# Last MLP chunk of a two-layer decoder trunk: two weight sums built in a second buffer, and the first product's weights moved to the staging buffer

## The chip, the core and the metric

One core of a Trainium2 chip runs the whole program. TensorE (PE) multiplies 128x128 weight tiles with up to 512 columns, VectorE (DVE) and ScalarE (ACT) do elementwise work, GpSimd (POOL) does some of it and issues DMAs that add to their destination, SyncE (SP) issues plain DMAs. The engines are ordered only by semaphores. The metric is the device time of one launch in microseconds.

## The reference

Two layers, 512 tokens, width 1024, all float32. Each layer has a token mixer (dilated attention and retention, merged by gates) and then an MLP, which is what matters here:

```python
h2 = rmsnorm(x, g_ffn)                                    # 512 x 1024
x = x + jnp.square(jax.nn.relu(h2 @ w_up)) @ w_down       # w_up 1024 x 4096, w_down 4096 x 1024
```

After the second layer a last RMSNorm makes the output.

## The kernel before

Every float32 product is made of three products of float32r operands: a value is split into a high part (a cast, on ACT) and a low part (value minus high part, on DVE), and PE adds high x high, low x high and high x low. Weights come in **units** of 128x2048 float32 (1 MB). A unit is loaded to a staging buffer `raw`, cast by ACT in two halves to `w_hi[n % 2]`, and DVE subtracts two halves into `w_lo[n % 2]`. The semaphore `lo_done` counts these halves. As there are two pairs `w_hi`/`w_lo`, the cast for unit n+1 may begin when unit n-1 is multiplied, that is when PE begins unit n. `raw` is single: the DMA of a half waits for the `lo_done` of the same half of the unit that used `raw` last (`load`, with `raw_before`).

The MLP is cut along the 4096 hidden columns into 4 chunks, c = 0 to 3. For a chunk, four U units make `us[c % 2]`, the squared ReLU (8 tiles of 512 columns, so 128x4096 float32), and the product with the chunk's 1024x1024 part of `w_down` is made by 7 block products D1 to D7 instead of 8, from sums of quarter blocks. With q(h, m) a quarter of the weights (`w_down_q[l, c, h, m]`, 1 MB), the weights that each product uses are:

- D1: q(0,0). D5: q(0,0)+q(0,1). D6: that + q(1,1). D4: that + q(1,0).
- D3: q(1,1). D7: q(1,1)+q(0,1).
- D2: q(1,0), which is the only one that goes through `raw`.

The first two rows are built in place in two buffers, `gh[0]` and `gh[1]`: SP loads the first quarter (`sum_slot`), ACT and DVE split it for its product, and when DVE is done POOL issues an accumulating DMA (`add_quarter`) that adds the next quarter to the buffer; then the next product's weights are split from it, and so on. POOL's DMAs stand in its program in a fixed order; for each chunk: the one for D5 (behind D1's split), for D6 (behind D5's), for D7 (behind D3's), for D4 (behind D6's).

The order of units (`M_SEQ`) interleaves the D products of chunk c with the U units of chunk c+1. The end of chunk 2 and the last chunk have no U units between them: D7 of chunk 2, U3, D2, D4 of chunk 2, and then, for chunk 3, `DOWN_LAST` = D1, D2, D5, D3, D6, D7, D4, each 24 matmuls of 512 columns. In the last chunk each product is done in two token halves (`down_halves`), each evicted on its own by DVE (`evict_half`, which adds the PSUM bank to an accumulator `acc`). PE begins D3 only when the first half of D5 is evicted, D7 when that of D6 is, D4 when that of D7 is, since they share PSUM banks (`down_ready`).

DVE's program for one unit of the last chunk is, in order: evict the second half of the unit before, split the weights of the unit after (`weights_low`), make the low parts of an activation operand (`a_low`), evict the first half of the own unit, and after D5 one sum of activations (`sum_of`). ACT's is: cast the weights of the unit after (`weights_high`), cast an activation operand (`a_high`). SP's program around this: the U loads of chunk 3, the first quarter for D1 of chunk 3, the load for D2 of chunk 2, the first quarter for D3 of chunk 3, the load for D2 of chunk 3, and then the next layer's first weights.

Of the kernel before, what the change touches and what calls it, by code (L numbers as in the profile page):

```python
# [52 lines left out]
def trunk(nc, a):  # L53
# [44 lines left out]
    LD = len(D_SEQ)  # L98
    LA = 2 * LD

    def by_raw(j):
        return j < M0 or M_SEQ[j - M0][0] == "U" or M_SEQ[j - M0][2] == 2

    RAW = [j for j in range(LU) if by_raw(j)]

# [7 lines left out]
    def m_unit(l, kind, c, i):  # L113
        return l * LU + M0 + M_SEQ.index((kind, c, i))

    def d_no(c, i):
        return D_SEQ.index((c, i))
# [7 lines left out]
    def slot_of(l, c, as_sum):  # L125
        return (l * CH + c) % 2 if as_sum else 1 - (l * CH + c) % 2

    def adds_before(l, c, as_sum):
        w, s = l * CH + c, slot_of(l, c, as_sum)
        return w // 2 * 4 + ((3 if s == 0 else 1) if w % 2 else 0)  # L130

    with ExitStack() as ctx:
        def sb(name, shape, dt):
# [5 lines left out]
        def sem(name):  # L139
            return ctx.enter_context(nc.semaphore(name))  # L140
# [95 lines left out]
            a_sets[r] = (at("M", f"a_hi{r}", [P, 4, 2 * P], F32R), at("M", f"a_lo{r}", [P, 4, 2 * P], F32R))  # L236
        acc = [at("M", "acc0", [P, TB, S], F32), tables]
        us = [at("M", f"u{i}", [P, KT, S], F32) for i in range(2)]
        assert top["M"] == pad
        top["res_lo"], top["res_hi"] = zone0, zone0 + 3 * KT * S * 4  # L240
        res_hi = at("res_hi", "res_hi", [P, KT, S], F32R)
# [152 lines left out]
        u_done = sem("u_done")  # L394
        sum_in = [sem(f"sum_in{i}") for i in range(2)]
        sum_added = [sem(f"sum_added{i}") for i in range(2)]
        a_sum = sem("a_sum")
        a_hi_done = sem("a_hi_done")
        a_ready = sem("a_ready")
# [59 lines left out]
        def _(sp):  # L459
# [35 lines left out]
            for l in range(0, DEPTH):  # L495
# [135 lines left out]
                for i in range(0, 2):  # L631
                    for u in range(O_U):
                        load(l * LU + O0 + i * O_U + u, cols(w_o_u[l], 2 * i + u))
                def quarter(c):
                    d = raw[:].rearrange("p (k c) -> p k c", k=4)
                    return [(d[:, m:m + 2, :], w_down_q[l, c, 1, 0][:, m:m + 2, :]) for m in (0, 2)]

                def sum_slot(c, as_sum):
                    w, slot = l * CH + c, slot_of(l, c, as_sum)
# [17 lines left out]
                for c in range(CH):  # L657
                    if c < CH - 1:
                        up_weights(c + 1, 1)
                        up_weights(c + 1, 2)  # L660
                        up_weights(c + 1, 3)
                        sum_slot(c + 1, True)
                    load(m_unit(l, "D", c, 2), quarter(c))
                    if c < CH - 2:
                        up_weights(c + 2, 0)
                    if c < CH - 1:
                        sum_slot(c + 1, False)
# [9 lines left out]
        def _(act):  # L677
# [9 lines left out]
                    nc.scalar.copy(w_hi[s][:, c], raw[:, c]).then_inc(hi_done, 1)  # L687

            def hi_sum(l, c, i, n):
                slot = slot_of(l, c, i in (1, 5, 6, 4))  # L690
                adds = {1: 0, 5: 1, 6: 2, 4: 3, 3: 0, 7: 1}[i]
                if adds == 0:
                    act.wait_ge(sum_in[slot], (l * CH + c) * 16 + 16)
                else:
                    act.wait_ge(sum_added[slot], (adds_before(l, c, i in (1, 5, 6, 4)) + adds) * 16)
                for h in HALVES:
                    nc.scalar.copy(w_hi[n % 2][:, h], gh[slot][:, h]).then_inc(hi_done, 1)  # L697
# [75 lines left out]
            for l in range(0, DEPTH):  # L773
# [215 lines left out]
                def weights_high(j):  # L989
                    n = l * LU + M0 + j  # L990
                    act.wait_ge(mm_done, n * 2 - 2 + MM_CREDIT)
                    if j < len(M_SEQ):
                        kind, c, i = M_SEQ[j]
                        if kind == "D" and i != 2:
                            hi_sum(l, c, i, n)
                            return
                    hi_halves(n, n % 2)
# [94 lines left out]
        @block.gpsimd  # L1092
        def _(pool):
            nc.gpsimd.memset(ones[:], 1.0).then_inc(const_set, 1)
            nc.gpsimd.memset(inv_d[:], 1.0 / D).then_inc(const_set, 1)
            nc.gpsimd.memset(eps[:], EPS).then_inc(const_set, 1)
            nc.gpsimd.memset(shares[:], 0.0).then_inc(const_set, 1)
            for l in range(0, DEPTH):
                for i in range(0, PAIRS):
                    J = l * PAIRS + i  # L1100
                    q = l * LQ + i * P_U
                    for u in range(4):
                        for o in range(2):
                            pool.wait_ge(bank_free[o], q + u + 1 + BANK_CREDIT)
                            pool.wait_ge(rot_out, J * 8 + 2 * u + o + 1)
                            pool.wait_ge(tables_done, l + 1)
                            nc.gpsimd.tensor_tensor(rcos[:], rot[:], cosA if u < 3 else cosR,  # L1107
                                                    ALU.mult).then_inc(rot_cos, 1)

                def add_quarter(c, behind, as_sum, h, m):  # L1110
                    slot = slot_of(l, c, as_sum)
                    pool.wait_ge(lo_done, m_unit(l, "D", c, behind) * 2 + 2 + UNIT_CREDIT)
                    pool.wait_ge(sum_in[slot], (l * CH + c) * 16 + 16)
                    nc.gpsimd.dma_start(gh[slot][:].rearrange("p (k c) -> p k c", k=4), w_down_q[l, c, h, m],  # L1114
                                        accum_op=ALU.add).then_inc(sum_added[slot], 16)

                for c in range(CH):
                    add_quarter(c, 1, True, 0, 1)
                    add_quarter(c, 5, True, 1, 1)
                    add_quarter(c, 3, False, 0, 1)  # L1120
                    add_quarter(c, 6, True, 1, 0)


        @block.vector
        def _(dve):
# [108 lines left out]
            for l in range(0, DEPTH):  # L1234
# [350 lines left out]
                def weights_low(j):  # L1585
                    n = l * LU + M0 + j
                    if j < len(M_SEQ):
                        kind, c, i = M_SEQ[j]
                        if kind == "D" and i != 2:
                            for hf in range(2):  # L1590
                                lo_half(n, n % 2, hf, gh[slot_of(l, c, i in (1, 5, 6, 4))])
                            return
                    lo(n, n % 2)

# [73 lines left out]
                for j, (kind, c, i) in enumerate(M_SEQ):  # L1668
                    last_chunk = kind == "D" and c == CH - 1
                    if j > 0:  # L1670
                        before = M_SEQ[j - 1]
                        if before[0] == "U":
                            relu_square(before[1], before[2], 1)
                        elif before[1] == CH - 1:
                            evict_half(before[2], 1)
                        else:
                            evict(before[1], before[2])
                    if kind == "U" and c > 0:
                        for t in ((5,), (3,), (7,), ())[i]:
                            sum_of(c - 1, t)  # L1680
                    if last_chunk and i == 2:
                        sum_of(c, 3)
                    if j + 1 < len(M_SEQ) or not last_layer:
                        weights_low(j + 1)
                    if j == 0:
                        rms_squared(l)
                    if kind == "U" and c > 0:
                        for t in ((5,), (3, 6), (7, 2), (4,))[i]:
                            a_low(c - 1, t)
                        if i == 0:  # L1690
                            sum_of(c - 1, 6)
                    if (kind, i) in (("U", 2), ("U", 3)) and (c == 0) == (i == 2):
                        a_low(c, 1)
                    if (kind, c, i) == ("U", 0, 2) and last_layer:
                        gains_diag()
                    if (kind, c, i) == ("D", CH - 2, 2):
                        sum_of(CH - 1, 5)
                    if (kind, c, i) == ("D", CH - 2, 4):
                        a_low(CH - 1, 2)
                        sum_of(CH - 1, 6)  # L1700
                    if last_chunk:
                        for t in {1: (5,), 2: (3,), 5: (6,), 3: (7,), 6: (4,)}.get(i, ()):
                            a_low(c, t)
                        if i != 4:
                            evict_half(i, 0)
                        if i == 5:
                            sum_of(c, 7)
                    if kind == "U":
                        relu_square(c, i, 0)
                    if last_chunk and last_layer and i == 7:  # L1710
                        f_add(0, 2, 4)
                        f_inverse(0, 2, 1)
                        dve.wait_ge(g_kept, 2)
                        f_scaled(0, 1)
                        f_scaled(0, 0)
# [542 lines left out]
```

## Time and profile before

| | us |
|---|---|
| median of 3 runs (lowest, highest) | 1888.55 (1887.93, 1889.95) |
| the profiled execution | 1888.48 |
| its span in the trace | 1886.4 |
| PE busy in it | 1865.5 (99%) |
| DVE / ACT / POOL busy | 1255.6 / 837.2 / 129.4 |

The span runs from the first to the last instruction of the trace. The profile's times below are microseconds from the span's start. A MATMUL row shows 0.39 us, but matmuls overlap: at full clock their starts are 0.23 us apart, so a D product takes 5.44 us and the gap between one row's start and the next shows a stall. Layer 0's last chunk runs from 896.21 us, layer 1's from 1834.79 us.

### The profile page before, as it was taken

Reading aid. Unit: us, or ns where it says so; the run is one execution under the profiler, and the core shown is the slowest. Engines: PE = TensorE matmul, PEld = TensorE weight load, DVE = VectorE, ACT = ScalarE, POOL = GpSimd, SP = SyncE. Lnnn points to the kernel's source line nnn. Section 1 sums busy time; section 2 is a strip of 40 time slices with the busy share of each in tenths; the row PEclk is TensorE's granted clock in tenths of the full one; section 3 lists DMA queues with packets and bytes.
Section 4 is the critical chain, followed back from the end, with each engine's and each line's share of the span. In section 5 each row is a group of like instructions: output and inputs, shape, how many; then the busy total and the mean of one; then the engine's idle time right before and its main releaser. Section 6 shows DMA issues by size and latency. Waiting matters only on the chain.

```text
span 1886.4 us, 22990 instructions
## 1 busy us (share of the span) xinstructions
PE 1865.5 (99%) x9064; PEld 1549.7 (82%) x9064; DVE 1255.6 (67%) x1858; ACT 837.2 (44%) x1234; POOL 129.4 (7%) x104
## 2 busy tenths in 40 slices
PE   9999999999999999999899999999999999999997
PEld 7888888887888888888788888888878888888886
DVE  5356778767456666767863568788665575676777
ACT  7325465464223333434472255554632233344344
POOL 0001111100000000000000112111000000000100
PEclk9999999999999999999999999999999999999999
DMA  4543233333333465564626333233243334655655
GB/s 146 200 159 120 83 89 118 90 93 104 120 101 114 132 134 136 150 136 125 145 88 240 96 104 104 77 118 104 68 146 101 101 112 113 141 148 134 134 147 121
DMA packets 208235, 230.64 MB, mean 122 GB/s; under 512 B 13440, under 2 KB 160640, under 8 KB 207360
## 3 DMA queue, kind: packets, MB, share of 16 engines
q1 hardware_dynamic: 190512, 194.74, 32.7%
q0 software_dynamic: 16896, 33.56, 10.5%
q8 instruction: 72, 1.18, 0.2%
q10 hardware_dynamic: 720, 0.87, 0.1%
q14 instruction: 35, 0.29, 0.0%
HBM read 215.38 MB, written 13.77 MB: 121 GB/s over the span
## 4 chain that ended last, share of the span: by engine, by line
PE 85%; issue 6%; DVE 4%; DMA 3%; ACT 2%; POOL 0%; SPq 0%; POOLq 0%; ACTq 0%; DVEq 0%
PE pj L1816 19%; PE pj L1818 19%; PE pj L1817 19%; DMA gh<-in_w_down 2%; PE yr L2122 1%; PE yr L2124 1%; PE yr L2126 1%; DVE w_lo L1140 1%; PE pt L2122 1%; PE pt L2124 1%; PE pt L2126 1%; PE sc L2122 1%; PE sc L2124 1%; PE sc L2126 1%; PE yr L1923 1%
## 5 line engine op out<-in xcount | busy, mean ns | idle before, releaser
L1816 PE MATMUL pj<-h_hi,w_hi 128*128 128x512 f32 x1408 | 554.4, 394 | 1.0 <-DVE sA L1515 1.0
L1818 PE MATMUL pj<-h_hi,w_lo 128*128 128x512 f32 x1408 | 548.5, 390 | 0.0
L1817 PE MATMUL pj<-h_lo,w_hi 128*128 128x512 f32 x1408 | 548.3, 389 | 0.0
L1140 DVE TENSOR_TENSOR w_lo<-w_raw,w_hi 128x1024 fp32r<-128x1024 f32 x279 | 329.9, 1220 | 115.1 <-ACT w_hi L687 113.6
L687 ACT CAST w_hi<-w_raw 128x1024 fp32r<-128x1024 f32 x276 | 278.6, 1049 | 270.5 <-PE pj L1818 56.9
L1816 PEld LDWEIGHTS pj<-h_hi,w_hi 128*128 128x128 f32 x1408 | 264.4, 188 | 59.0 <-issue 1.9
L1818 PEld LDWEIGHTS pj<-h_hi,w_lo 128*128 128x128 f32 x1408 | 264.3, 188 | 56.0
L1817 PEld LDWEIGHTS pj<-h_lo,w_hi 128*128 128x128 f32 x1408 | 264.5, 188 | 53.9 <-issue 0.5
L697 ACT CAST w_hi<-gh 128x1024 fp32r<-128x1024 f32 x96 | 96.0, 1050 | 118.2 <-DMA gh<-in_w_down 50.5
L1107 POOL TENSOR_TENSOR rcos<-rot,tables 128x512 f32<-128x512 f32 x64 | 87.6, 1370 | 692.4 <-ACT rot L808 633.8
L1140 DVE TENSOR_TENSOR w_lo<-gh,w_hi 128x1024 fp32r<-128x1024 f32 x96 | 113.1, 1219 | 14.2 <-ACT w_hi L697 14.0
L975 ACT ACTIVATE relu<-pj 128x512 f32<-128x512 f32 x64 | 38.2, 597 | 189.6 <-PE pj L1818 189.6
L1581 DVE TENSOR_TENSOR u<-relu,rstd_all 128x512 f32<-128x512 f32 x64 | 44.0, 688 | 105.5 <-ACT relu L975 105.5
L1114 POOL DMA_DIRECT2D gh<-in_w_down x32 | 41.2, 1286 | 1038.4 <-DVE w_lo L1140 1038.4
L808 ACT COPY rot<-pj 128x512 f32<-128x512 f32 x48 | 27.9, 582 | 110.5 <-PE pj L1818 64.5
L2122 PE MATMUL sc<-w_hi,a_hi 128*128 128x512 f32 x160 | 63.3, 396 | 5.7 <-DVE a_lo L1623 3.4
L1288 DVE TENSOR_TENSOR swp<-swp,tables 128x512 f32<-128x512 f32 x64 | 65.4, 1022 | 4.4 <-ACT swp L812 2.7
L2126 PE MATMUL sc<-w_hi,a_lo 128*128 128x512 f32 x160 | 63.0, 394 | 0.0
L2124 PE MATMUL sc<-w_lo,a_hi 128*128 128x512 f32 x160 | 62.9, 393 | 0.0
L2122 PE MATMUL yr<-w_hi,a_hi 128*128 128x512 f32 x160 | 62.2, 389 | 0.0
L2124 PE MATMUL yr<-w_lo,a_hi 128*128 128x512 f32 x160 | 62.2, 389 | 0.0
L2126 PE MATMUL yr<-w_hi,a_lo 128*128 128x512 f32 x160 | 62.2, 389 | 0.0
(339 smaller groups left out, 3102.4 us busy)
## 6 DMA issues: line engine op xcount, KB each, us to landing
w_raw<-in_w_in SPq DMA_DIRECT2D x151, 512.0 KB, 4.7
w_raw<-in_w_up SPq DMA_DIRECT2D x64, 512.0 KB, 4.9
gh<-in_w_down POOLq DMA_DIRECT2D x32, 1024.0 KB, 8.7
gh<-in_w_down SPq DMA_DIRECT2D x16, 1024.0 KB, 5.1
w_raw<-in_w_b SPq DMA_DIRECT2D x16, 512.0 KB, 3.9
w_raw<-in_w_o SPq DMA_DIRECT2D x16, 512.0 KB, 3.9
w_raw<-in_w_down SPq DMA_DIRECT2D x16, 512.0 KB, 4.5
x_scratch<-x SPq DMA_DIRECT2D x2, 2048.0 KB, 10.1
```

The source lines that it names most:

```text
L687: nc.scalar.copy(w_hi[s][:, c], raw[:, c]).then_inc(hi_done, 1)
L697: nc.scalar.copy(w_hi[n % 2][:, h], gh[slot][:, h]).then_inc(hi_done, 1)
L1107: nc.gpsimd.tensor_tensor(rcos[:], rot[:], cosA if u < 3 else cosR, ALU.mult).then_inc(rot_cos, 1)
L1140: nc.vector.tensor_tensor(w_lo[s][:, c], src[:, c], w_hi[s][:, c], ALU.subtract).then_inc(lo_done, 1)
L1288: nc.vector.tensor_tensor(swp[:], swp[:], sinA if u < GROUPS else sinR, ALU.mult).then_inc(rot_sin, 1)
L1581: nc.vector.tensor_tensor(to, relu[:, o, :], rstd_all[:], ALU.mult).then_inc(relu_scaled, 1)
L1816: nc.tensor.matmul(out, w_hi[s][:, wc], acts[0], start=first, stop=False)
L1817: nc.tensor.matmul(out, w_hi[s][:, wc], acts[1], start=False, stop=False)
L1818: return nc.tensor.matmul(out, w_lo[s][:, wc], acts[0], start=False, stop=last)
L2122: nc.tensor.matmul(out, hi[:, k, t], w_hi[s][:, w], start=opens and k == 0, stop=False, skip_group_check=not opens)
L2124: nc.tensor.matmul(out, hi[:, k, t], w_lo[s][:, w], start=False, stop=False, skip_group_check=not opens)
L2126: return nc.tensor.matmul(out, lo[:, k, t], w_hi[s][:, w], start=False, stop=k == 3, skip_group_check=not opens)
```

## The change

It touches the last chunk of each layer only.

- `us[0]`, which held chunk 2's activations, has no use in the last chunk. Its two halves of 1 MB become `spares[7]` and `spares[4]`.
- The weights of D7 and D4 of chunk 3 are built there: SP loads q(1,1) to `spares[7]` and q(0,0) to `spares[4]` when the last operand has been made from `us[0]` (D4 of chunk 2), and POOL adds one quarter to the first and three to the second, each waiting for the one before it.
- D1 of chunk 3 (q(0,0)) is loaded to `raw` like D2, right after D2 of chunk 2, and is so counted among the `raw` users. `gh[...]` with q(0,0) serves D5 and D6 only, with two adds, and the first of them does not wait for D1's split. D3's buffer has no add.
- POOL's order for chunk 3 is: add for D5, first add of `spares[4]`, the add of `spares[7]`, second and third add of `spares[4]`, add for D6.
- In DVE's program for the last chunk the eviction of the own unit's first half goes ahead of `a_low`.

```diff
+    def plain(c, i):
+        return i == 2 or (c, i) == (CH - 1, 1)
+
     def by_raw(j):
-        return j < M0 or M_SEQ[j - M0][0] == "U" or M_SEQ[j - M0][2] == 2
+        return j < M0 or M_SEQ[j - M0][0] == "U" or plain(*M_SEQ[j - M0][1:])
...
+        spare = us[(CH - 2) % 2]
+        spares = {7: spare[:, 0:4, :].rearrange("p k c -> p (k c)"), 4: spare[:, 4:8, :].rearrange("p k c -> p (k c)")}
...
-                    load(m_unit(l, "D", c, 2), quarter(c))
+                    load(m_unit(l, "D", c, 2), quarter(c, 1))
+                    if c == CH - 2:
+                        load(m_unit(l, "D", c + 1, 1), quarter(c + 1, 0))
+                        sp.wait_ge(a_ready, l * LD + d_no(c, 4) + 1)
+                        for i, src in ((7, w_down_q[l, c + 1, 1, 1]), (4, w_down_q[l, c + 1, 0, 0])):
+                            sp.dma_start(spares[i].rearrange("p (k c) -> p k c", k=4), src).then_inc(spare_in[i], 16)
...
             def hi_sum(l, c, i, n):
+                if c == CH - 1 and i in (7, 4):
+                    act.wait_ge(spare_added[i], (l + 1) * 16 * {7: 1, 4: 3}[i])
+                    for h in HALVES:
+                        nc.scalar.copy(w_hi[n % 2][:, h], spares[i][:, h]).then_inc(hi_done, 1)
+                    return
...
                 def add_quarter(c, behind, as_sum, h, m):
                     slot = slot_of(l, c, as_sum)
-                    pool.wait_ge(lo_done, m_unit(l, "D", c, behind) * 2 + 2 + UNIT_CREDIT)
+                    if not plain(c, behind):
+                        pool.wait_ge(lo_done, m_unit(l, "D", c, behind) * 2 + 2 + UNIT_CREDIT)
                     pool.wait_ge(sum_in[slot], (l * CH + c) * 16 + 16)
...
-                for c in range(CH):
+                def add_spare(i, n, h, m):
+                    if n == 0:
+                        pool.wait_ge(spare_in[i], l * 16 + 16)
+                    else:
+                        pool.wait_ge(spare_added[i], (l * 3 + n) * 16)
+                    nc.gpsimd.dma_start(spares[i].rearrange("p (k c) -> p k c", k=4), w_down_q[l, CH - 1, h, m],
+                                        accum_op=ALU.add).then_inc(spare_added[i], 16)
+
+                for c in range(CH - 1):
                     add_quarter(c, 1, True, 0, 1)
                     add_quarter(c, 5, True, 1, 1)
                     add_quarter(c, 3, False, 0, 1)
                     add_quarter(c, 6, True, 1, 0)
+                add_quarter(CH - 1, 1, True, 0, 1)
+                add_spare(4, 0, 0, 1)
+                add_spare(7, 0, 0, 1)
+                add_spare(4, 1, 1, 1)
+                add_spare(4, 2, 1, 0)
+                add_quarter(CH - 1, 5, True, 1, 1)
...
                     if last_chunk:
+                        if i != 4:
+                            evict_half(i, 0)
                         for t in {1: (5,), 2: (3,), 5: (6,), 3: (7,), 6: (4,)}.get(i, ()):
                             a_low(c, t)
-                        if i != 4:
-                            evict_half(i, 0)
```

Left out: the semaphores `spare_in` and `spare_added`, `adds_before` with the new counts, and the places where DVE and ACT ask `plain(c, i)` instead of `i == 2`, and DVE takes `spares[i]` as the source for D7 and D4.

## Rows read from the trace of the kernel before

**Rows 1.** The page: busy time, share, instructions.

```profile
PE 1865.5 (99%) x9064; PEld 1549.7 (82%) x9064; DVE 1255.6 (67%) x1858; ACT 837.2 (44%) x1234; POOL 129.4 (7%) x104
```

**Rows 2.** Timeline of PE, layer 0: first matmuls of D2 D5 D3 D6 D7 D4.

```profile
901.65 0.39 PE L2122 MATMUL yr<-w_hi,a_hi 128*128 128x512 f32 x1
907.09 0.39 PE L2122 MATMUL pt<-w_hi,a_hi 128*128 128x512 f32 x1
...
914.41 0.47 PE L2122 MATMUL pt<-w_hi,a_hi 128*128 128x512 f32 x1 [1.72 <-DVE a_lo L1623]
919.98 0.39 PE L2122 MATMUL sc<-w_hi,a_hi 128*128 128x512 f32 x1
927.15 0.47 PE L2122 MATMUL sc<-w_hi,a_hi 128*128 128x512 f32 x1 [1.57 <-DVE a_lo L1623]
934.35 0.47 PE L2122 MATMUL sc<-w_hi,a_hi 128*128 128x512 f32 x1 [1.48 <-DVE tables L1647]
```

**Rows 3.** Timeline of DVE: a_lo of D4 (chunk 2) and D1; D1's split; D5's eviction.

```profile
879.90 2.35 DVE L1623 TENSOR_TENSOR a_lo<-u,a_hi 128x1024 fp32r<-128x1024 f32 x2
...
892.17 2.35 DVE L1140 TENSOR_TENSOR w_lo<-gh,w_hi 128x1024 fp32r<-128x1024 f32 x2
...
913.64 0.68 DVE L1647 TENSOR_TENSOR tables<-tables,pt 128x512 f32<-128x512 f32 x1
```

**Rows 4.** Timeline of POOL: adds for D5, D6, D7, D4.

```profile
894.82 1.28 POOL L1114 DMA_DIRECT2D gh<-in_w_down  x1 [41.47 <-DVE w_lo L1140]
908.08 1.28 POOL L1114 DMA_DIRECT2D gh<-in_w_down  x1 [11.98 <-DVE w_lo L1140]
912.88 1.28 POOL L1114 DMA_DIRECT2D gh<-in_w_down  x1 [3.51 <-DVE w_lo L1140]
920.80 1.30 POOL L1114 DMA_DIRECT2D gh<-in_w_down  x1 [6.64 <-DVE w_lo L1140]
```

**Rows 5.** Timeline of ACT: D6's cast and D7's.

```profile
916.84 2.00 ACT L697 CAST w_hi<-gh 128x1024 fp32r<-128x1024 f32 x2 [6.60 <-DMA gh<-in_w_down]
...
921.88 2.01 ACT L697 CAST w_hi<-gh 128x1024 fp32r<-128x1024 f32 x2 [2.08 <-DMA gh<-in_w_down]
```

**Rows 6.** The chain of waits: start, us, what.

```profile
863.04 4.94 DMA gh<-in_w_down
...
920.80 9.34 DMA gh<-in_w_down
```

**Rows 7.** The page, DMA issues: xcount, size, median us to landing.

```profile
gh<-in_w_down POOLq DMA_DIRECT2D x32, 1024.0 KB, 8.7
```

**Rows 8.** Timeline of SP: D2's load (chunk 2); D3's quarter; D2's load.

```profile
872.42 1.50 SPq L475 DMA_DIRECT2D w_raw<-in_w_down  x2
889.88 0.37 SPq L645 DMA_DIRECT2D gh<-in_w_down  x1
890.31 1.00 SPq L475 DMA_DIRECT2D w_raw<-in_w_down  x2
```

**Rows 9.** DMA view of 852 to 864 us, 40 slices of 0.3 us.

```profile
GB/s 0 0 0 0 0 0 20 75 55 102 177 184 205 198 198 191 205 198 218 212 212 218 218 171 263 181 266 335 386 386 379 386 382 382 362 215 10 0 0 0
...
w_raw<-in_w_up SPq DMA_DIRECT2D x2, 512.0 KB, 6.9
```

**Rows 10.** Timeline of SP and POOL: what was issued in that window.

```profile
852.07 1.28 POOL L1114 DMA_DIRECT2D gh<-in_w_down  x1 [9.23 <-DVE w_lo L1140]
...
855.33 1.56 SPq L475 DMA_DIRECT2D w_raw<-in_w_up  x2
```

**Rows 11.** Timeline of PE, layer 1: D7, two later matmuls, D4's second half.

```profile
1865.67 0.47 PE L2122 MATMUL sc<-w_hi,a_hi 128*128 128x512 f32 x1 [1.86 <-DVE a_lo L1623]
...
1867.94 0.63 PE L2122 MATMUL sc<-w_hi,a_hi 128*128 128x512 f32 x1
1868.37 0.63 PE L2124 MATMUL sc<-w_lo,a_hi 128*128 128x512 f32 x1
...
1876.52 0.50 PE L2122 MATMUL sc<-w_hi,a_hi 128*128 128x512 f32 x1 [0.83 <-DVE tables L1647]
```

More of the change, by code:

```diff
@@ L126, in slot_of, with adds_of @@
         return (l * CH + c) % 2 if as_sum else 1 - (l * CH + c) % 2
+    def adds_of(c, as_sum):
+        return (2 if as_sum else 0) if c == CH - 1 else (3 if as_sum else 1)
     def adds_before(l, c, as_sum):
-        w, s = l * CH + c, slot_of(l, c, as_sum)
-        return w // 2 * 4 + ((3 if s == 0 else 1) if w % 2 else 0)
+        slot = slot_of(l, c, as_sum)
+        return sum(adds_of(w % CH, slot_of(0, w, True) == slot) for w in range(l * CH + c))
     with ExitStack() as ctx:
@@ L396, in trunk @@
         sum_added = [sem(f"sum_added{i}") for i in range(2)]
+        spare_in = {i: sem(f"spare_in{i}") for i in (7, 4)}
+        spare_added = {i: sem(f"spare_added{i}") for i in (7, 4)}
         a_sum = sem("a_sum")
@@ L633, in _, with quarter @@
                         load(l * LU + O0 + i * O_U + u, cols(w_o_u[l], 2 * i + u))
-                def quarter(c):
+                def quarter(c, h):
                     d = raw[:].rearrange("p (k c) -> p k c", k=4)
-                    return [(d[:, m:m + 2, :], w_down_q[l, c, 1, 0][:, m:m + 2, :]) for m in (0, 2)]
+                    return [(d[:, m:m + 2, :], w_down_q[l, c, h, 0][:, m:m + 2, :]) for m in (0, 2)]
                 def sum_slot(c, as_sum):
@@ L993, in weights_high @@
                         kind, c, i = M_SEQ[j]
-                        if kind == "D" and i != 2:
+                        if kind == "D" and not plain(c, i):
                             hi_sum(l, c, i, n)
@@ L1588, in weights_low @@
                         kind, c, i = M_SEQ[j]
-                        if kind == "D" and i != 2:
+                        if kind == "D" and not plain(c, i):
                             for hf in range(2):
-                                lo_half(n, n % 2, hf, gh[slot_of(l, c, i in (1, 5, 6, 4))])
+                                lo_half(n, n % 2, hf, spares[i] if c == CH - 1 and i in (7, 4) else
+                                        gh[slot_of(l, c, i in (1, 5, 6, 4))])
                             return
```

## The prediction

> **What bounds the kernel now.** The page says PE: busy 1865.5 us [rows 1] of a span of 1886.4. So a change can only win where PE stands still. I read PE's own timeline next. A D product is 24 matmuls; D2 and D5 begin 5.44 us apart (901.65, 907.09), which is the unstalled pitch [rows 2]. After them D3 begins at 914.41 where 912.53 was due, a stall of 1.88; D6 at 919.98 (as it should, 5.57 later); D7 at 927.15, 7.17 after D6, a stall of 1.73; D4 at 934.35, 7.20 after D7, a stall of 1.76 [rows 2]. Unstalled, D4 would begin at 901.65 + 5 x 5.44 = 928.85, so this layer's last chunk holds 5.5 us that can be won.
>
> What ends those waits? For D3 the reader must not stop at the releaser: the last thing was the eviction of D5's first half, at 913.64 for 0.68 us [rows 3]; that half was multiplied by 907.09 + 2.72 = 909.8 already, and DVE was behind with other work. For D4 the chain of waits shows POOL's add issued at 920.80 and 9.34 us to its landing at 930.14 [rows 6], though PE had begun D7 at 927.15 and ACT could have cast D4's weights from then on. For D6 ACT waited for a DMA until 916.84, for D7 until 921.88 [rows 5]: these sums arrive just in time or somewhat late. In layer 1 D7 begins at 1865.67 after 1.86 us of standing, and a while later the matmuls start 0.43 us apart instead of 0.23: the granted clock is at the 1.2 GHz level there [rows 11]. Layer 0, with stalls of the same size, shows no such drop.
>
> **What DMAs cost here.** An accumulating DMA of 1 MB takes 8.7 us from issue to landing, alone [rows 7]. Two in a row: the adds issued at 908.08 and 912.88 [rows 4] landed where ACT's casts begin, 916.84 and 921.88 [rows 5], that is 5.1 us apart. So one occupies the DMA engines for 5.1 us, and the one behind it lands 5.1 us after it. A plain load moves about 386 GB/s in the DMA view where an accumulating one moves about 205 [rows 9]; 1.05 MB / 386 is 2.7 us of the engines, and it lands 4.94 after its issue [rows 6]. The same view shows what both do together: the accumulating DMA was issued at 852.07, two halves of a plain load from 855.33 on [rows 10]; the rate stays near 205 until about 859 and is 386 only from 860.4 on, and the plain halves took 6.9 us to land [rows 9]. The two do not overlap to any gain: their times on the engines add, and the plain load stood behind the whole accumulating one.
>
> **The change part by part.** Times are those of layer 0; layer 1 lies 938.5 later (D7 927.15, 1865.67).
>
> (a) Add for D5. It was issued at 894.82 behind D1's split [rows 4]; now it waits only for its first quarter, landed at 863.04 + 4.94 = 868.0 [rows 6]. POOL had been idle for 41.47 us before 894.82 [rows 4], so it goes at 868 and occupies the engines from about 870 to 875.5. That covers D2 of chunk 2's load, issued at 872.42 [rows 8], which slips by some 1.2 us. PE needs it only for 885.33 on my count (three products before 901.65: 901.65 - 3 x 5.44), so it costs PE nothing. But DVE's split of it, and with it the a_lo pair that starts at 879.90 [rows 3], slips by 1.2 too.
>
> (b) `spares`. SP waits for the first of that pair: 879.90 + 1.2 + 1.2 = 882.3. In front are the two halves of D1's load, issued when D2's halves are split, with 2.7 us of transfer ending near 884.1. Then two plain MB: 884.1 + 2 x 2.7 = 889.5, landing near 890.0.
>
> (c) POOL's queue, the heart of it. From 890 the DMA engines get: D3's quarter, issued at 889.88 as before [rows 8] (2.7); first add to `spares[4]`, issued at 890.0 (5.1); the add to `spares[7]`, issued one POOL instruction, 1.28 us [rows 4], later (5.1); D2's load (2.7). The first add lands at 890.0 + 8.7 + 2.1 for the part of D3's quarter in front of it = 900.8, the one for D7 at 905.9. The second add to `spares[4]` may be issued only at 900.8 and finds D7's add and D2's load before it: 900.8 + 5.1 + 2.7 + 5.1 = 913.7. The third is issued at 913.7, and **only behind it in POOL's program comes the add for D6**, which was issued at 908.08 before. The third has idle engines, 8.7, and lands at 922.4; D6's add lands 5.1 later, at 927.5. Before, it landed at 916.8.
>
> (d) D2's load. It used `raw` behind chunk 2's D2 and was issued at 890.31 [rows 8]; now `raw` holds D1's weights until DVE has split them, 892.17 to 894.52 [rows 3], so its halves go at 893.4 and 894.6, among POOL's adds. The engines' work listed in (c) is 15.6 us from 891.7 on, so the second half lands at up to 908. Cast (1.0), split (1.2) and handovers make 2.4 us to 910.5, and PE can do D2's last three quarters after that: it ends at 910.5 + 0.75 x 5.44 = 914.6 where it ended at 907.09. A PE stall of 7.5 us. D5 then begins at 915.6 (its split stands behind D2's in DVE's program), D3 near 922 and ends near 928. The Trainium skill, "DMA: Bandwidth & Descriptors", Queues, rings and completion order, says that each DMA engine goes round between the queues at packet granularity, 9 to 17 descriptors typically; by that rule D2's second half would land at 905.5 and D2 end at 912. In the window above no such switch is seen. It changes nothing in the sum, only the margin by which (e) decides instead of (d).
>
> (e) PE after the change. D6 begins 2.4 us after its sum landed, at 929.9 (D3 is done at 928). D7 waits for the eviction of D6's first half, which in DVE's program stands behind D6's second split (1.1), eviction, a_lo, eviction, D7's split (0.7 + 1.1 + 0.7 + 2.35), and takes 0.7: 6.7 us, so D7 begins at 936.6. D4's weights have been there since 922.4 and its split and the eviction of D7's first half fit in D7's 5.44 us: D4 begins at 942.0 without a stall. Before it was 934.35: **7.7 us late**. What follows D4 (turns, the next layer, in layer 1 the last norm with D4's second half at 1876.52 behind DVE [rows 11]) hangs on D4's start by the same work as before.
>
> (f) The eviction ahead of `a_low`: would give D3 the 1.14 us of one DVE instruction of that size (half of 2.35 [rows 3]). It lies in the shadow of (c): 0. D5's add, D7's and D4's sums come in time, and are worth 0 too, since D6 stands before them.
>
> (g) Clock. A stall of 1.86 us was followed by a drop in one layer and not in the other; stalls of 5 to 7 us make a drop likelier. With the drop of [rows 11] D7 took from 1865.67 to about 1873.0, 7.3 instead of 5.44, so at most 1.9 us a drop; at least 0, as D2's drop has D3's margin of 2 us to vanish in. Between 0 and 3 us in all; I take 0.5.
>
> Sum: 2 x 7.7 + 0.5 = 15.9 on the profiled execution's 1888.48 (its span 1886.4 and 2.1 around it); the median shown is 1888.55, the same within 0.1. That is 1904.
>
> **Rivals.**
>
> *It does what it is built for: 1878.* If the three adds and the two spares were done soon enough, all stalls from D3 to D4 go: 5.5 in layer 0 and in layer 1 as much (D4 began about 1873.0 there: 1876.52 less the stall of 0.83 and half a product, 2.72 [rows 11]; unstalled 938.5 + 928.85 = 1867.4); 1888.5 - 11 = 1877.5, say 1878. For it: D5's, D7's and D4's sums are in truth taken off the path. Against: D6's add stands last in POOL's order and cannot be issued before two further adds have landed one after the other; it needs accumulating DMAs that cost the engines half of what [rows 5] show.
>
> *No contention: 1892.* If (a)'s slip is nil and neither D3's quarter nor D2's load delays POOL's adds: first add 888.8 + 8.7 = 897.5, D7's 902.6, second 907.7, third 916.4, D6's 921.5; D6 begins at 923.9, D7 at 930.6, D4 at 936.0, 1.7 late; 1888.5 + 3.4 = 1892. With D7's wait for DVE gone as well, 1.3 less a layer, 1889. Against it: the plain megabytes must go through the same engines [rows 9].
>
> *Plain loads starve: 1920.* If POOL's queue is served first as long as it has work, D3's quarter and D2's load go only in the gaps of POOL's chain; D2's second half would land near 919, D5's split be done near 928, D6's add (it waits for that) be issued there and land at 937: D6 at 939.3, 9.4 later than in (e), twice: 1904 + 19 = 1923, less if one half slips in. For it: [rows 9], where the plain load waits for the whole accumulating one. Against: one waiting behind another that began first is no priority.
>
> **Chances.** The forecast's case, 1897 to 1912: 0.62. Faster, 1878: 0.12. No contention: 0.13, of which half lies within 0.2% (3.8 us, about what a measurement of this kernel can tell from no change). Starving: 0.10; the rest anything else. So faster 0.12, same 0.08, slower 0.80. The range leaves out the case of 1878 and the worst of starving: 1889 to 1915.
>
> **What would show it.** Right: on POOL two adds near 900.8 and 913.7 and then at once D6's; D6's cast near 927 waiting for that DMA; PE standing for 5 to 8 us in or before D2 with the w_raw cast behind a DMA; D3's eviction no longer what PE waits for; D4 without a wait. Wrong: adds landing 5 us after their issue; D2's cast near 897 as before; D6's wait on D3's end. If D5's add is not seen near 868, (a) is wrong and with it the time of everything behind it.

## The result and the profile after

| | before | changed |
|---|---|---|
| median of 4 runs each, us (lowest, highest) | 1888.24 (1887.38, 1889.95) | 1914.14 (1912.96, 1914.91) |
| the profiled execution, us | 1888.48 | 1914.91 |
| its span, us | 1886.4 | 1912.8 |
| ratio to before, 95% interval | | 1.0135 (1.0118 to 1.0153) |

The changed kernel is 26 us slower. The forecast was 1904, range 1889 to 1915: the median lies inside the range by 0.9 us and above 1897 to 1912, which the prediction called the forecast's own case.

Where the 26.4 us of span are. PE's timeline of layer 0's last chunk, first matmuls of D2, D2's second quarter (the first to need the second half of its weights), D5, D3, D6, one later matmul, D4 (the numbers in brackets are us of waiting and the releaser); [rows 2] are their like:

```profile
901.11 0.39 PE L2158 MATMUL yr<-w_hi,a_hi 128*128 128x512 f32 x1
...
905.40 0.50 PE L2158 MATMUL yr<-w_hi,a_hi 128*128 128x512 f32 x1 [2.77 <-DVE w_lo L1175]
...
910.09 0.47 PE L2158 MATMUL pt<-w_hi,a_hi 128*128 128x512 f32 x1 [0.31 <-DVE w_lo L1175]
...
916.38 0.47 PE L2158 MATMUL pt<-w_hi,a_hi 128*128 128x512 f32 x1 [0.59 <-issue]
...
935.13 0.76 PE L2158 MATMUL sc<-w_hi,a_hi 128*128 128x512 f32 x1 [12.74 <-DVE w_lo L1175]
...
936.97 0.63 PE L2160 MATMUL sc<-w_lo,a_hi 128*128 128x512 f32 x1
...
947.67 0.39 PE L2158 MATMUL sc<-w_hi,a_hi 128*128 128x512 f32 x1
```

From D2's start to D4's it was 32.7 us [rows 2] and is 46.6: 13.9 lost. The largest piece is the wait of 12.74 ahead of D6; the shorter waits in D2, D5 and D3 (3.7 together) and the slow matmuls behind D6's (1.7) come to about what the old stalls had cost, 5.5. D4 follows without a wait, as does D7. Why D6 waits is read on POOL: the add for D5, the two first spare adds (`u<-` is the dead buffer), the second and the third to `spares[4]`, the add for D6 (`gh<-` again):

```profile
867.88 1.28 POOL L1135 DMA_DIRECT2D gh<-in_w_down  x1 [15.07 <-DMA gh<-in_w_down]
893.60 2.59 POOL L1143 DMA_DIRECT2D u<-in_w_down  x2 [24.44 <-DMA u<-in_w_down]
907.03 1.30 POOL L1143 DMA_DIRECT2D u<-in_w_down  x1 [10.84 <-DMA u<-in_w_down]
919.05 1.29 POOL L1143 DMA_DIRECT2D u<-in_w_down  x1 [10.71 <-DMA u<-in_w_down]
919.79 1.85 POOL L1135 DMA_DIRECT2D gh<-in_w_down  x1
```

and on ACT, D2's two casts and D6's:

```profile
897.34 1.05 ACT L702 CAST w_hi<-w_raw 128x1024 fp32r<-128x1024 f32 x1 [3.95 <-DMA w_raw<-in_w_down]
903.04 1.04 ACT L702 CAST w_hi<-w_raw 128x1024 fp32r<-128x1024 f32 x1 [4.65 <-DMA w_raw<-in_w_down]
...
932.68 1.99 ACT L717 CAST w_hi<-gh 128x1024 fp32r<-128x1024 f32 x2 [19.88 <-DMA gh<-in_w_down]
```

The load of D2's second half stands on SP at:

```profile
894.01 0.37 SPq L485 DMA_DIRECT2D w_raw<-in_w_down  x1
```

The add for D6 was issued at 908.08 [rows 4] and is at 919.79, less than a microsecond behind the third spare add. Of these 11.7 us D5's own lateness explains 3.3 (its split ended at 911.08, 907.79 before); for the rest the add stands behind two landings in POOL's program. The chain of waits (start, us, what) now runs over these DMAs:

```profile
883.62 9.71 DMA u<-in_w_down
...
893.60 12.95 DMA u<-in_w_down
...
919.79 12.81 DMA gh<-in_w_down
```

In layer 1 it is the same picture, smaller (POOL's two first spare adds, the second, the third, the add for D6):

```profile
1848.57 2.62 POOL L1143 DMA_DIRECT2D u<-in_w_down  x2 [23.55 <-DMA u<-in_w_down]
1861.06 1.28 POOL L1143 DMA_DIRECT2D u<-in_w_down  x1 [9.86 <-DMA u<-in_w_down]
1871.17 1.28 POOL L1143 DMA_DIRECT2D u<-in_w_down  x1 [8.84 <-DMA u<-in_w_down]
1871.92 1.84 POOL L1135 DMA_DIRECT2D gh<-in_w_down  x1
```

There D2 waits 4.39 and D6 7.46, and from D1's start (1851.46) to D4's second half it takes 51.5 us where it took 41.7, 9.8 lost. The rest is a wait that the change does not touch in the code, a gate unit (weights of the token mixer's gates) in layer 1, with a matmul pitch of 0.43 behind it. First D2, D6 and D4's second half of layer 1, then that unit:

```profile
1862.82 0.50 PE L2158 MATMUL yr<-w_hi,a_hi 128*128 128x512 f32 x1 [4.39 <-DVE w_lo L1175]
...
1887.20 0.76 PE L2158 MATMUL sc<-w_hi,a_hi 128*128 128x512 f32 x1 [7.46 <-DVE w_lo L1175]
...
1902.98 0.50 PE L2158 MATMUL sc<-w_hi,a_hi 128*128 128x512 f32 x1 [0.25 <-DVE tables L1683]
```

```profile
1408.23 0.50 PE L1852 MATMUL pj<-h_hi,w_hi 128*128 128x512 f32 x1 [2.26 <-DVE sA L1550]
...
1410.33 0.63 PE L1853 MATMUL pj<-h_lo,w_hi 128*128 128x512 f32 x1
```

13.9 + 9.8 + 3.3 there (1.7 of wait more than the 0.59 that this unit waited before, and 8 matmuls 0.2 us longer each), less 0.5 by which this execution ran ahead before the chunk, is the 26.4 to within 0.2.

### The profile page after: what moved, and what is told of

It reads as the page before. It is cut to its first block, busy times and chain, and to the rows that moved or that the text cites. A ratio compares the mean times of both kernels' runs of the same rounds, so it can differ in the third digit from the quotient of the medians.

```text
span 1912.8 us, 22996 instructions
## 1 busy us (share of the span) xinstructions
PE 1871.6 (98%) x9064; PEld 1553.4 (81%) x9064; DVE 1255.5 (66%) x1858; ACT 836.8 (44%) x1234; POOL 134.9 (7%) x108
## 4 chain that ended last, share of the span: by engine, by line
PE 87%; DMA 5%; DVE 3%; ACT 2%; issue 2%; POOL 0%; SPq 0%; ACTq 0%; DVEq 0%; POOLq 0%
PE pj L1852 19%; PE pj L1854 19%; PE pj L1853 19%; DMA u<-in_w_down 2%; PE sc L2158 1%; PE sc L2160 1%; PE sc L2162 1%; PE yr L2158 1%; PE yr L2160 1%; PE yr L2162 1%; DMA gh<-in_w_down 1%; PE pt L2158 1%; PE pt L2162 1%; PE pt L2160 1%; DVE w_lo L1175 1%
## 5 line engine op out<-in xcount | busy, mean ns | idle before, releaser
L1175 DVE TENSOR_TENSOR w_lo<-w_raw,w_hi 128x1024 fp32r<-128x1024 f32 x283 | 334.9, 1220 | 134.8 <-ACT w_hi L702 133.4
L702 ACT CAST w_hi<-w_raw 128x1024 fp32r<-128x1024 f32 x280 | 282.7, 1049 | 296.1 <-PE pj L1854 56.9
L717 ACT CAST w_hi<-gh 128x1024 fp32r<-128x1024 f32 x84 | 83.9, 1049 | 109.9 <-DMA gh<-in_w_down 52.4
L1175 DVE TENSOR_TENSOR w_lo<-gh,w_hi 128x1024 fp32r<-128x1024 f32 x84 | 99.0, 1220 | 24.1 <-ACT w_hi L717 23.8
L1135 POOL DMA_DIRECT2D gh<-in_w_down x28 | 37.1, 1325 | 944.5 <-DVE w_lo L1175 914.3
```

Of the source, the lines that this page charges most:

```text
L1175: nc.vector.tensor_tensor(w_lo[s][:, c], src[:, c], w_hi[s][:, c], ALU.subtract).then_inc(lo_done, 1)
```

## Experiments

Times are medians; ratios are to the kernel before, run beside each on the same chip (its medians there: 1887.65 to 1888.28). "Before" and "changed" in the table say which of the two kernels was edited.

| kernel | us | ratio, 95% interval |
|---|---|---|
| changed | 1914.14 | 1.0135 (1.0118 to 1.0153) |
| e2: changed, D6's add ahead of the third spare add | 1895.21 | 1.0041 (1.0026 to 1.0056) |
| e4: changed, D1 in gh again | 1920.45 | 1.0177 (1.0161 to 1.0192) |
| e8: e2 and e4 together | 1902.02 | 1.0073 (1.0057 to 1.0088) |
| e5: changed, no spare adds (sums incomplete) | 1880.46 | 0.9966 (0.9955 to 0.9978) |
| e9: changed, next layer's weights later | 1910.99 | 1.0123 (1.0109 to 1.0136) |
| e3: before, D1 through raw | 1889.84 | 1.0008 (0.9998 to 1.0018) |
| e1: before, evictions ahead of a_low | 1887.59 | 0.9998 (0.9989 to 1.0007) |
| e6: e1, D4's sum in the dead buffer | 1893.48 | 1.0027 (1.0016 to 1.0039) |
| e7: e1, D6's sum in the dead buffer | 1896.28 | 1.0044 (1.0031 to 1.0056) |
| e10: before, two evictions ahead of the split | 1886.78 | 0.9996 (0.9987 to 1.0005) |

**e2, the order on POOL.**

```diff
                 add_spare(4, 1, 1, 1)
-                add_spare(4, 2, 1, 0)
                 add_quarter(CH - 1, 5, True, 1, 1)
+                add_spare(4, 2, 1, 0)
```

> The changed kernel with one line moved: POOL issues the add for D6 ahead of the third add to spares[4], not behind it. Theory (POOL's order): D6's add is then issued when D5 is split, near 911 us of layer 0, and lands near 923 instead of 932.6; D6 begins near 925.5 instead of 935.1, the third add lands near 929 and D4 follows without a long wait: about 9 us a layer back, 1896. Rival (D2's late load and the busy DMA engines set the end): D6's add lands only 2 or 3 us earlier, since the bytes ahead of it are the same, and the time stays at 1908 or more.

Measured 1895.21: two lines exchanged give 19 us back. POOL's timeline of e2, the second spare add, D6's, the third:

```profile
906.89 1.30 POOL L1143 DMA_DIRECT2D u<-in_w_down  x1 [10.95 <-DMA u<-in_w_down]
912.67 1.29 POOL L1135 DMA_DIRECT2D gh<-in_w_down  x1 [4.47 <-DVE w_lo L1175]
919.38 1.28 POOL L1143 DMA_DIRECT2D u<-in_w_down  x1 [5.42 <-DMA u<-in_w_down]
```

D6's add now waits for DVE's split of D5, as it was meant to, and ACT's cast of D6 began at 924.24. The rival (the same bytes ahead, so 2 or 3 us) is out: the place in POOL's program counted, worth 19 of the 26 us.

**e4, D1 in gh again.**

```diff
-        return i == 2 or (c, i) == (CH - 1, 1)
+        return i == 2
...
-                        load(m_unit(l, "D", c + 1, 1), quarter(c + 1, 0))
```

> The changed kernel with D1's weights of the last chunk taken from gh again, so that D2's load goes early and the add for D5 waits for D1's split; both spares and POOL's order stay. Theory (POOL's order): the stall in D2 (3.2 us in layer 0, 4.8 in layer 1) goes, but D6's sum still lands near 932, so the end hardly moves: 1911 to 1916. Rival (D2's late load carries the loss): 4 to 8 us a layer come back, 1900 to 1906.

Measured 1920.45, slower than either theory had it. PE's timeline of e4, D2, D5, D3, D6:

```profile
901.15 0.39 PE L2157 MATMUL yr<-w_hi,a_hi 128*128 128x512 f32 x1
...
906.60 0.39 PE L2157 MATMUL pt<-w_hi,a_hi 128*128 128x512 f32 x1
...
912.26 0.47 PE L2157 MATMUL pt<-w_hi,a_hi 128*128 128x512 f32 x1
...
938.03 0.77 PE L2157 MATMUL sc<-w_hi,a_hi 128*128 128x512 f32 x1 [19.81 <-DVE w_lo L1174]
```

D2's stall is gone, and D6 begins 2.9 us later than in the changed kernel. Taking the stall in D2 away gave nothing back. What costs more instead is read on POOL (the add for D5, the two first spare adds, the second):

```profile
894.32 1.28 POOL L1134 DMA_DIRECT2D gh<-in_w_down  x1 [41.47 <-DVE w_lo L1174]
895.06 3.15 POOL L1142 DMA_DIRECT2D u<-in_w_down  x2
912.05 1.30 POOL L1142 DMA_DIRECT2D u<-in_w_down  x1 [13.83 <-DMA u<-in_w_down]
```

The add for D5, at 894.32 instead of 868, stands in front of the spare adds, and the second of these goes out 5.0 us later than in the changed kernel. D1 through raw, with the early add that it allows, saves 6 us in all; that the early add is what saves them is read from these rows, and no run moves it alone. Some of the 6 is clock: behind the longer wait 13 matmuls start 0.43 us apart, 7 in the changed kernel.

**e8, both edits.**

> The changed kernel with both of two edits tried alone before: D1's weights in gh again, and D6's add ahead of the third spare add. Theory (D6 is set by when POOL can issue its add, which is behind the landing of the second spare add's predecessor, not by D2): with the add for D5 in front at 894 the second spare add is issued near 912 and D6's at 913.3, landing near 923, as with the new order alone: 1893 to 1898. Rival (D2's stall and the order each cost their part, and the parts add): 1888 or less.

Measured 1902.02, above the theory's 1893 to 1898 and the rival's 1888: the expectation failed. The order gives 19 us with D1 in raw (1914.14 to 1895.21) and 18 with it in gh (1920.45 to 1902.02); D1 in raw saves 6 us in one order and 7 in the other. The two add up, with the sign of the second opposite to the rival's. Where the theory failed is D6's landing, put at 923: its cast began at 927.28, since its add, issued at 912.78 as expected, went out right behind the second spare add at 912.03 (in e2 5.8 us behind it).

**e5, the spare adds left out.** Of the sums for D7 and D4 only one quarter is there.

```diff
-                    act.wait_ge(spare_added[i], (l + 1) * 16 * {7: 1, 4: 3}[i])
+                    act.wait_ge(spare_in[i], (l + 1) * 16)
...
-                add_spare(4, 0, 0, 1)
-                add_spare(7, 0, 0, 1)
-                add_spare(4, 1, 1, 1)
-                add_spare(4, 2, 1, 0)
```

> The changed kernel without the four accumulating DMAs into the spares: D7 and D4 take one plain quarter each, so the result leaves out parts of their sums. Everything else, the plain loads to the spares and D2's late load among it, stays. Theory (the chain of spare adds in front of D6's add): D2's load lands near 899 and stalls nothing much, D6's add is issued when D5 is split and lands near 917, no product waits for more than 1 us, D4 begins near 928.5: 1878. Rival (the plain loads to the spares and D1 through raw cost on their own): above 1890.

Measured 1880.46, 2.5 us above the theory's figure and far from the rival's. So the four adds a layer cost the changed kernel 34 us in all. With them gone it is 8 us faster than the kernel before, plain loads to the spares and D1 through raw included: that is what lay to be won had the adds been free (11 by my rival's sum). It issues two adds a layer in the last chunk where the kernel before issues four, so some of the 8 us may be work that no full kernel can leave out. Even here D3 and D7 began late behind a DVE eviction, by 0.2 and 0.8 us. ACT's timeline of e5, D2's two casts and D6's:

```profile
897.56 1.05 ACT L702 CAST w_hi<-w_raw 128x1024 fp32r<-128x1024 f32 x1 [3.91 <-DMA w_raw<-in_w_down]
899.11 1.06 ACT L702 CAST w_hi<-w_raw 128x1024 fp32r<-128x1024 f32 x1 [0.50 <-DMA w_raw<-in_w_down]
...
915.99 2.00 ACT L717 CAST w_hi<-gh 128x1024 fp32r<-128x1024 f32 x2 [6.03 <-DMA gh<-in_w_down]
```

The second of D2's halves is there 3.9 us earlier than in the changed kernel, where spare adds are under way beside it.

**e9, another megabyte out of the way.**

```diff
                     if c < CH - 1:
                         sum_slot(c + 1, False)
+                if l < DEPTH - 1:
+                    sp.wait_ge(lo_done, m_unit(l, "D", CH - 1, 6) * 2 + 2 + UNIT_CREDIT)
```

> The changed kernel, with the next layer's first weights (1 MB, which go out while the spare adds run in layer 0) held back until D6's weights are split. Theory (every megabyte in front of D6's add delays it by its time on the DMA engines): D6's sum in layer 0 lands 2.5 to 3.5 us earlier, layer 1, which has no such load, stays: 1911. Rival (only the order of POOL's landings counts, plain loads fit between): no change, 1914.

Measured 1910.99, 3 us less, but the two ratios' intervals overlap, so the medians alone do not tell it from the changed kernel. The profiled executions do: the third spare add of layer 0 goes out at 917.30 instead of 919.05 and D6's cast at 931.24 instead of 932.68, while D1 had begun 0.45 later than there, so 1.9 us are won in this place. The changed kernel's own layer 1, which has no next layer to load for, says the same: its second spare add is followed by the third 10.1 us later (1861.06, 1871.17), in layer 0 it takes 12.0 (907.03, 919.05). The direction is the theory's, the size less than its 2.5 to 3.5 us.

**e3, D1 through raw alone.** The changed kernel's `plain`, its load of D1 and its early add for D5, on the kernel before; no spares.

> The kernel before with one part of the change: D1 of the last chunk through raw, and the add for D5 at once; no spares, D7's and D4's sums in their old buffers, the eviction in its old place. Theory: D2's load goes at 893 but finds free engines and lands near 898.5, no stall; D5's split can be 2.5 us earlier and with it D6's add and split, and so D4's add, which bounds D4: 0 to 2 us a layer won, 1885 to 1888. Rival (D1 through raw makes D2 late by itself): 2 or more lost a layer, 1892 or more.

Measured 1889.84, the interval holds 1: no change, 2 us above what the theory had. The second half of D2 was cast at 899.63, in time; but the add for D6 was issued at 908.17, as before (908.08), so an earlier D5 sum moved nothing. DVE no longer waited for it, but D2's second half was split at 900.71, 1.7 us later than before, and the work behind that pushed D5's split to 905.51, where it had been (905.43).

**e1, the evictions alone.**

```diff
+                        if i != 4:
+                            evict_half(i, 0)
                         for t in {1: (5,), 2: (3,), 5: (6,), 3: (7,), 6: (4,)}.get(i, ()):
                             a_low(c, t)
-                        if i != 4:
-                            evict_half(i, 0)
```

> The kernel before with one part of the change: in DVE's program for the last chunk the eviction of the own unit's first half goes ahead of a_low. Theory (a product waits for the later of its sum and the eviction): D3 and D7 begin 1.1 us earlier each, D7 then bound by its sum, which lands at 921.9; D4's sum still lands near 930.1, so D4 begins as before: within 1 us, 1887 to 1888.5. Rival (each eviction moved earlier moves the end): 2 us a layer won, 1884.

Measured 1887.59, no difference: within the theory's range, away from the rival's. PE's timeline of e1, D3, D7, D4:

```profile
912.63 0.47 PE L2122 MATMUL pt<-w_hi,a_hi 128*128 128x512 f32 x1 [0.37 <-issue]
...
925.56 0.47 PE L2122 MATMUL sc<-w_hi,a_hi 128*128 128x512 f32 x1 [1.29 <-issue]
...
932.83 0.47 PE L2122 MATMUL sc<-w_hi,a_hi 128*128 128x512 f32 x1 [1.55 <-DVE tables L1647]
```

D3 begins 11.4 us after D2 (12.8 before [rows 2]), D4 31.6 after it (32.7 before): of 1.4 us won at D3, 1.1 is left at D4, and of that nothing that the medians can tell.

**e6 and e7, one spare only.** Both have D1 in gh and e1's evictions. e6 builds D4's sum in the dead buffer, e7 D6's, with D4's made in the old buffer right after D5. POOL's order in e7, where the last wait is for the add before it in `gh`, and D4's second add follows:

```diff
                 add_spare(0, 0, 1)
                 add_quarter(c, 1, True, 0, 1)
                 add_spare(1, 1, 1)
                 add_quarter(c, 5, True, 1, 1)
                 add_quarter(c, 3, False, 0, 1)
                 pool.wait_ge(sum_added[slot], (adds_before(l, c, True) + 2) * 16)
...
```

> The kernel before with the eviction first and only D4's sum built in the dead buffer, three adds, in POOL's order: first spare add, D5's, second spare add, D6's, D7's, third spare add; D1 stays in gh, D7's sum stays in its old buffer. Theory (an add delays what stands behind it by 5.1 us of the DMA engines, and by the landing that POOL waits for): D6's add is issued near 909 and lands near 918, D7's near 923, the third spare add near 928: D4 begins 2 us earlier than before, 1884. Rival (any spare adds ahead of D6's cost more than they bring): 1890 or more.

> The kernel before with the eviction first and only D6's sum built in the dead buffer (two adds), D4's in the buffer of D5 by two adds right after D5's split, so that no add waits for D6's split; POOL's order: first spare add, D5's, second spare add, D4's first, D7's, D4's second. Theory: D6's sum lands near 909, D7's near 922, D4's near 927; D3 and D6 begin on time, D7 within 1.5 us and D4 within 1.5 us of unstalled: 4 us a layer won, 1880. Rival (the DMA engines are too busy with one more megabyte and one more add): the adds land 5 us later than that and nothing is won, 1887 or more.

Measured 1893.48 and 1896.28: both theories failed, at the same place, and both times lie where the rivals had them. ACT's timeline of e7, D2's two casts:

```profile
900.14 1.05 ACT L694 CAST w_hi<-w_raw 128x1024 fp32r<-128x1024 f32 x1 [6.40 <-DMA w_raw<-in_w_down]
903.96 1.05 ACT L694 CAST w_hi<-w_raw 128x1024 fp32r<-128x1024 f32 x1 [2.77 <-DMA w_raw<-in_w_down]
```

D2's load was issued at 890.12, where it always was, and behind D3's quarter as always; new ahead of it is the first spare add (886.85). Before, the first cast was at 896.67. PE stood for 0.96 and 2.10 us in D2 (2.17 and 2.41 in e6), D5's split came 4 to 7 us later than before, and D6's or D4's add with it: D4 started 36 us after D1's end in both, where it had been 32.7. I had counted what the spare add does to the adds behind it, and not to D2's plain load.

**e10, DVE's order without any spare.** For D6 and D7 the eviction of the first half goes ahead of the split of the next weights.

```diff
+                    if last_chunk and i in (6, 7):
+                        evict_half(i, 0)
                     if j + 1 < len(M_SEQ) or not last_layer:
                         weights_low(j + 1)
...
```

The other products' evictions stand ahead of `a_low`, as in e1.

> The kernel before, with no spares and its own adds; only DVE's program changes: the eviction of D6's and of D7's first half goes ahead of the split of the next product's weights, that of the others ahead of a_low. Theory (with the sums landing near 921.4 and 928.7, D7 and D4 wait for an eviction that stands behind the whole split): D7 begins when D6 ends, near 924.0 instead of 925.6 with the eviction only ahead of a_low, and D4 near 931.0 (landing 928.7 plus one half cast and split) instead of 932.8: 3 us a layer before the kernel before, 1884. Rival (D4's sum sets D4 and DVE has no part in it): as with the eviction ahead of a_low alone, 1887.5.

Measured 1886.78; the interval holds 1, and of the 4 us forecast at most 1 is there. That is nearer to the rival's 1887.5 than to the theory's 1884. In layer 0 it did what it should: D7 follows D6 with no wait, and D4 stands only for its own split, 30.25 us after D2 instead of 32.7:

```profile
931.24 0.47 PE L2124 MATMUL sc<-w_hi,a_hi 128*128 128x512 f32 x1 [1.34 <-DVE w_lo L1140]
```

In layer 1 D4 began 30.9 us after D2 instead of 32.6, and lost it again:

```profile
1867.88 0.76 PE L2124 MATMUL sc<-w_hi,a_hi 128*128 128x512 f32 x1 [2.71 <-DVE w_lo L1140]
...
1873.79 0.50 PE L2124 MATMUL sc<-w_hi,a_hi 128*128 128x512 f32 x1 [1.48 <-DVE tables L1647]
```

Its sum arrived no earlier, so PE stood 2.71 us for it; 8 matmuls behind that wait start 0.43 us apart, the 1.7 us that the kernel before lost in D7 [rows 11]; and its second half waited 1.48 us for D7's second eviction (0.83 before), which on DVE stands behind work of the last norm. That half began 36.8 us after D2, 36.3 before. So this is the fastest of the kernels that compute the whole, and not one that a measurement tells from the kernel before.

## Why the prediction held

The sign, the place and the mechanism were right, the size was short: 15.9 us forecast, 26 measured (26.4 of span in the profiled execution). Of the 10.5 us between 15.9 and 26.4, layer 0 holds 6.2 (13.9 against 7.7), layer 1 2.1 (9.8 against 7.7), and 3.3 are the gate unit's, which the prediction does not have; against these go the 0.5 of clock that (g) had in the sum and the 0.5 of the earlier start. That the time still fell into the range owes something to its width.

- (a) held in its main point: the add for D5 went out at 867.88, 868 forecast.
- (c) was the heart, and e2 shows it: D6's add behind two landings and a third add. Its parts, forecast and measured in layer 0: spare loads landed 890.0 and 893.3; second spare add issued 900.8 and 907.0; third 913.7 and 919.0; D6's sum landed 927.5 and 932.6. The first two links are 6.2 us late; from there to the end it took 26.7 and 25.6.
- That last agreement is partly luck. From the third add on the price was right, 13.8 us against 13.6 here and 13.5 in layer 1. The step before it was forecast at 12.9, with the add for D7 and D2's load in front; it took 12.0 in layer 0 beside the next layer's first weights, which the list in (c) left out, and 10.1 in layer 1 without them.
- The first late link: the two spare megabytes. I let them follow D1's load at the engines' pace. They took 9.7 us from issue, with D3's quarter (issued 889.34) beside them on SP's queue. They were also issued at 883.21 and not 882.3: (a)'s slip of D2's load of chunk 2 was not 1.2 but 2.6 us (DVE's a_lo pair at 881.96, after 0.5 for the earlier start of this execution).
- The second: from the first spare add to the next on its buffer it took 13.4 us and not 10.8. D2's load, which (c) put behind both adds, went out with them, its halves at 892.88 and 894.01, and the next layer's first megabyte began at 899.68. In layer 1, without the latter, it is 12.5, so most of the excess is not the next layer's. How much is D2's load's no run separates.
- (d) was wrong in size and in meaning. D2's first half left ahead of the adds; its second left at 894.01, 0.4 us behind the first spare add, and was cast at 903.04, not past 908, 3.5 us before that add landed. So the loads did not queue up behind whole adds as (d) added them; its other figure, by turns between the queues, was 905.5. PE stood 2.77 us in D2, not 7.5, and D5 began at 910.09, not 915.6. e4 removes the stall and the kernel becomes slower: it lay in D6's shadow, as (e) had it, and D1 through raw with its early add, which (f) priced at 0, was worth 6 us.
- (e): D6 to D4 12.1 us forecast, 12.5 measured, and that is luck too. The forecast had 1.3 us of D7 waiting for DVE's eviction and no clock in it; measured are no wait of D7 and 1.7 us of the clock at its 1.2 GHz level, behind which the eviction (over at 941.3, 6.2 us after D6's start) was in time.
- (g): the clock's 0.5 was small. In this execution it was low behind D6's wait in both layers, 1.7 us each, behind D2's in layer 1, which lies in D6's shadow, and once at the gate unit, where the loss with the wait was 3.3.
- The rivals: "no contention" fell at the spare loads; "starving" too, since D2's second half, issued after the first spare add, landed before it. The gain of "it does what it is built for" exists (e5, 8 us of the 11), at a price of adds that is not to be had.

Left open: the gate unit's wait of 2.3 us in layer 1. The longest wait at this line is 0.5 to 0.9 in the kernel before, e1, e2, e3, e6, e8 and e10, but 2.2 to 2.4 in the changed kernel, e4, e5, e7 and e9. e5 has it and is fast, e2 has not. In all five kernels that show it the profiled execution is above the kernel's median, by 0.8 to 2.9 us, and of the seven others five lie below it and two above by less than 0.7. So the wait may belong to the execution and not to the change; one trace a kernel does not show which, and nor do the experiments.

## What to carry to other kernels

In these runs a DMA that adds into a buffer was serial work: two queued ones landed 5.1 us apart [rows 5], and one that had to wait for the landing of the one before it went out 9 to 17 us after it. Count for each sum when its last add can be *issued*, in the program order of the issuing engine, before you count bytes: two lines exchanged were worth 19 us here. Taking a sum off another's buffer bought nothing here, as the longer chain was put in front of the one that was due first. Before adding transfers in a stretch where some arrive just in time, list the plain loads that they will stand in front of; e6 and e7 lost to those.

## What the runs showed of the hardware

One accumulating DMA in flight held a later plain load back until it was almost done [rows 9]. By queue, in the kernel before from 857 to 859 us, with the add issued at 852.07 and the plain halves from 855.33 on (packets, MB, share of the engines; q0 is POOL's queue, q1 SP's):

```profile
q0 software_dynamic: 195, 0.40, 108.8%
q1 hardware_dynamic: 2, 0.00, 0.4%
```

With more adds queued it was otherwise: in the changed kernel from 903 to 908 us both queues move, the total between the 205 of adds alone and the 386 of plain loads.

```profile
GB/s 197 180 279 229 262 246 279 246 295 246 279 279 229 311 246 279 246 279 262 262 262 262 262 262 262 262 262 262 262 262 262 262 262 180 246 229 229 180 197 197
...
q0 software_dynamic: 370, 0.73, 78.3%
q1 hardware_dynamic: 272, 0.52, 31.6%
```

Both queues got turns there, so neither has the priority that my third rival needed. "DMA: Bandwidth & Descriptors" of the Trainium skill, Queues, rings and completion order, has the engines go round between queues by packets; this window agrees as far as both queues move in it; the one of [rows 9] shows hardly a turn within one accumulating megabyte. Why the two differ stays open.

TensorE's clock was at its 1.2 GHz level behind most long waits and stayed there into the work that followed: in the changed kernel behind the waits of 12.74, 7.46, 4.39 and 2.26 us (granted 0.50 or 0.51 of full speed), but not behind the one of 2.77 (granted 1.00); in the kernel before behind one of 1.86 (0.50) [rows 11] and not behind those of layer 0. Eight matmuls or so then start 0.43 us apart, 1.7 us lost each time; in e4, behind waits of 19.81 and 17.35 us, it was 13 and 12 matmuls, 2.8 and 2.6 us.
